# Differential attention: which engine scales which half of the second softmax map, and in what order

## What is computed

```python
sc = einsum('bqhmd,bkhmd->bmhqk', q, k) * scale + bias     # m = 0, 1: two maps
p = softmax(sc, axis=-1)
a = p[:, 0] - lam * p[:, 1]
o = einsum('bhqk,bkhd->bqhd', a, v)
```

## Time and profile before

| | us |
|---|---|
| median of 3 executions | 4073.03 |
| lowest, highest | 4069.45, 4078.59 |
| the profiled execution, whole | 4074.67 |
| its span on the core | 4072.9 |

### The profile page before, as it was taken

One profiled execution on the slowest core, in us unless ns is written; L12 is line 12 of the kernel. 1 busy time (PEld: TensorE's weight loads), 2 busy tenths in 40 slices (PEclk: granted clock), 3 DMA queues, 4 the chain that ended last, 5 costly groups with the idle time before them and its releaser, 6 DMA issues. The chain is left out here.

```text
span 4072.9 us, 51499 instructions
## 1 busy us (share of the span) xinstructions
PE 3784.2 (93%) x19002; PEld 2622.2 (64%) x19002; DVE 2239.3 (55%) x3967; ACT 1658.5 (41%) x2882; POOL 2472.6 (61%) x1385
## 2 busy tenths in 40 slices
PE   8999999999989999789989999999999898997898
PEld 8788774555545665557777897755555465565587
DVE  3012125656569999775530021255555799997754
ACT  3112104333358888661031121033333588886610
POOL 1221326877769999755512213277777699996555
PEclk9999999999999999899989999999999999998999
DMA  5333534243220222335353335323322202224253
GB/s 178 124 134 116 161 122 114 67 101 75 61 56 1 56 57 52 79 89 187 129 181 126 129 120 156 127 59 75 74 65 57 56 3 55 56 52 102 81 179 128
DMA packets 179680, 391.38 MB, mean 96 GB/s; under 512 B 17854, under 2 KB 98984, under 8 KB 167784
## 3 DMA queue, kind: packets, MB, share of 16 engines
q1 hardware_dynamic: 178568, 386.70, 33.7%
q10 hardware_dynamic: 864, 1.41, 0.2%
HBM read 254.88 MB, written 135.67 MB: 96 GB/s over the span
## 5 line engine op out<-in xcount | busy, mean ns | idle before, releaser
L1279 POOL TENSOR_TENSOR mla_sum_pool<-mla_sum_pool,mla_probs 128x1024 f32<-128x1024 f32 (+1 forms) x336 | 777.6, 2314 | 209.5 <-ACT mla_probs L1240 184.7
L1297 DVE TENSOR_REDUCE carry_row_max<-psum 128x1 f32<-128x512 f32 x688 | 474.6, 690 | 415.7 <-PE psum L1112 410.9
L1240 ACT ACTIVATE mla_probs<-psum 128x1024 f32<-128x1024 f32 x384 | 373.3, 1021 | 694.2 <-PE psum L1149 689.5
L1589 ACT ACTIVATE diff_probs<-psum,diff_shift 128x1024 f32<-128x1024 f32 x512 | 566.1, 1111 | 186.3 <-DVE diff_shift L1671 180.3
L1664 DVE TENSOR_REDUCE diff_row_max<-psum 128x1 f32<-128x1024 f32 x512 | 611.9, 1218 | 44.5 <-PE psum L1510 37.2
L1536 PE MATMUL psum<-ident,diff_probs 128*128 128x128 f32 x2048 | 330.1, 285 | 105.8 <-DVE diff_turned L1698 72.0
L624 PE MATMUL psum<-in_x_hi,in_w_hi 128*128 128x512 f32 x1024 | 403.9, 394 | 2.7 <-ACT in_mla_val L733 2.7
L624 PE MATMUL psum<-carry_firsts,in_w_hi 128*128 128x512 f32 x1024 | 404.2, 395 | 0.0
L624 PE MATMUL psum<-in_x_hi,in_w_lo 128*128 128x512 f32 x1024 | 401.4, 392 | 0.0
L1536 PEld LDWEIGHTS psum<-ident,diff_probs 128*128 128x128 f32 x2048 | 217.3, 142 | 282.9 <-issue 185.7
L1162 PE MATMUL psum<-mla_probs,mla_v_op 128*64 128x512 f32 x1536 | 374.9, 610 | 0.0
(11 more groups left out here) (209 smaller groups left out, 7407.4 us busy)
## 6 DMA issues: line engine op xcount, KB each, us to landing
in_w_raw<-in_w_in SPq DMA_DIRECT2D x64, 512.0 KB, 3.9
split_d<-in_out SPq DMA_DIRECT2D x64, 512.0 KB, 2.6
raw_d<-in_out SPq DMA_DIRECT2D x32, 512.0 KB, 2.6
mq_d<-in_out SPq DMA_DIRECT2D x48, 256.0 KB, 3.4
mk_d<-in_out SPq DMA_DIRECT2D x48, 256.0 KB, 3.9
carry_firsts<-split_d SPq DMA_DIRECT2D x48, 256.0 KB, 8.0
carry_weights<-split_d SPq DMA_DIRECT2D x48, 256.0 KB, 7.7
carry_weights<-split_d SPq DMA_DIRECT2D x16, 768.0 KB, 17.2
```

Of the source, the lines that this page charges most:

```text
L1240: nc.scalar.activation(probs[:, s % RING, :].rearrange("p (a n) -> p a n", n=CH), psum[:, S0 + 2 * (s % 2):S0 + 2 * (s % 2) + 2, :], ACT.E ...
L1279: nc.gpsimd.tensor_tensor(acc, start, probs[:, s % RING, mine], ALU.add).then_inc(pool_added, 1)
L1297: nc.vector.tensor_reduce(row_max[:, u % 2, qb, n:n + 1], psum[:, sweep_bank(g), :], AX.X, ALU.max).then_inc(maxed, 1)
L1589: nc.scalar.activation(dst[:, half * HALF:(half + 1) * HALF].rearrange("p (a n) -> p a n", n=CH), banks(n, m, half), ACT.Exp, bias=shift[: ...
```

## The change

A constant `SCALED = HALF` sets how many columns ACT scales: 1024, the whole first half, and not 512. POOL has three instructions a unit and not four: it first scales the second half (which needs only `ratio`), then waits for ACT's scaling and adds the first half, then adds the second half. In the last two units POOL scales nothing and waits for ACT, which scales the 1024 columns alone. DVE's ratio of unit n waits for POOL's one multiply and for ACT's scaling of the unit two before.

```diff
--- before.py
+++ after.py
@@ -1394,6 +1394,7 @@
     DRAIN = 4
     LATE = UNITS - 2
     LOADS = 16 * 14
+    SCALED = HALF
     carry, carry_sems = carry
     vecs, lam_loaded = carry["vecs"], carry_sems["lam_loaded"]
     with ctx:
@@ -1593,7 +1594,7 @@
                 def scale(n):
                     act.wait_ge(ratio_ready, n + 1)
                     at = 0 if n < LATE else HALF
-                    first = probs1[:, n % DEEP1, at:at + CH]
+                    first = probs1[:, n % DEEP1, at:at + SCALED]
                     nc.scalar.activation(first, first, ACT.Copy, scale=ratio[:, n % 2:n % 2 + 1]).then_inc(act_scaled, 1)
 
                 def copy(n, c):
@@ -1635,23 +1636,18 @@
 
 
                     pool.wait_ge(ratio_ready, n + 1)
+                    if n < LATE:
+                        third = probs1[:, n % DEEP1, HALF:SEQ]
+                        nc.gpsimd.tensor_tensor(third, third, ratio[:, n % 2:n % 2 + 1].broadcast_to([P, HALF]), ALU.mult
+                                                ).then_inc(times_ratio, 1)
                     at = 0 if n < LATE else HALF
-                    done = 2 * n if n < LATE else LATE + n
-                    second = probs1[:, n % DEEP1, at + CH:at + HALF]
-                    nc.gpsimd.tensor_tensor(second, second, ratio[:, n % 2:n % 2 + 1].broadcast_to([P, HALF - CH]),
-                                            ALU.mult).then_inc(times_ratio, 1)
                     pool.wait_ge(act_scaled, n + 1)
-                    pool.wait_ge(times_ratio, done + 1)
                     nc.gpsimd.tensor_tensor(probs[:, n % DEEP, at:at + HALF], probs[:, n % DEEP, at:at + HALF],
                                             probs1[:, n % DEEP1, at:at + HALF], ALU.add).then_inc(mixed, 1)
-                    if n >= LATE:
-                        continue
-                    third = probs1[:, n % DEEP1, HALF:SEQ]
-                    nc.gpsimd.tensor_tensor(third, third, ratio[:, n % 2:n % 2 + 1].broadcast_to([P, HALF]), ALU.mult
-                                            ).then_inc(times_ratio, 1)
-                    pool.wait_ge(times_ratio, done + 2)
-                    nc.gpsimd.tensor_tensor(probs[:, n % DEEP, HALF:SEQ], probs[:, n % DEEP, HALF:SEQ], third, ALU.add
-                                            ).then_inc(mixed, 1)
+                    if n < LATE:
+                        pool.wait_ge(times_ratio, n + 1)
+                        nc.gpsimd.tensor_tensor(probs[:, n % DEEP, HALF:SEQ], probs[:, n % DEEP, HALF:SEQ], third, ALU.add
+                                                ).then_inc(mixed, 1)
 
                 pool.wait_ge(o_ready, (H - 1) * (NB // 2))
                 pool.wait_ge(mixed, LATE + UNITS)
@@ -1683,7 +1679,8 @@
                     nc.vector.reciprocal(inv1[:, n % 2:n % 2 + 1], totals[:, 1, qb, h:h + 1]).then_inc(inverted, 1)
                     dve.wait_ge(inverted, n + 1)
                     if n >= 2:
-                        dve.wait_ge(times_ratio, 2 * (n - 1))
+                        dve.wait_ge(times_ratio, n - 1)
+                        dve.wait_ge(act_scaled, n - 1)
                     nc.vector.tensor_scalar(ratio[:, n % 2:n % 2 + 1], inv1[:, n % 2:n % 2 + 1],
                                             totals[:, 0, qb, h:h + 1], dots[:, 0:1], ALU.mult, ALU.mult
                                             ).then_inc(ratio_ready, 1)
```

## The result

The changed kernel takes 4087.23 us (median of 7, 4084.1 to 4089.56), against 4073.03 (median of 7, 4069.45 to 4082.24) before: a ratio of 1.0028, 95% interval 1.0018 to 1.0037. It is slower, by 0.18 to 0.37%. The profiled execution took 4084.1 us, its span is 4082.3 (before: 4072.9). Run once more beside other kernels, it took 4086.8 us against 4078.4 of the kernel before, ratio 1.0023 (1.0014 to 1.0032). The median of the kernel before lay between 4073 and 4078 from one set of runs to the next, so differences are told here as ratios within a set, or from the traces. Within a set the longer executions mostly have the lower mean granted TensorE clock over the whole span (kernel before in the last set: 4067.15 us at 0.980, 4083.66 at 0.975); inside the steady part of the stage it is 1.00 in every trace.

What follows compares the result with a forecast made beforehand. POOL set the stage's long-run mean, with a DVE-PE loop of almost the same length. 24.9 us cost less 10.4 relief gave +14.5 on the profiled 4074.7, so 4089.2, or 4088 as a median; range 4082 to 4098.

Steps and rivals of the forecast that it cites:

- The steady part of the sum: First 28 head-sum distances per layer in the differential-attention stage; the whole forecast change, +14.5 us, was placed there.
- The ends: Last three head-sum distances of each layer, where the stage drains; forecast to change by nothing in sum.
- The scaling: ACT's scaling instruction, 1024 columns instead of 512: forecast to grow by 0.43 us, from 727 ns to 1.16 us.
- The idle time ahead of the head sum: Sign on DVE in each odd iteration: 0.3 to 0.4 us idle before L1716, released by ACT's odd half.
- 24.9 us: Cost of ACT's longer scaling delaying DVE's head sum once per odd iteration: 58 x 0.43 us; bounds 18.6 and 42.
- POOL's relief: Gain from POOL losing its 512-column multiply: 10.4 us, 8.4 in the pairs and about 2 at the layers' starts.
- The steps by which it was split over the pairs: Relief in iteration pairs: 0.5 us for the 15.58 us pair, 0.4 and 0.15 for those of 15.80 and 15.83.
- number 3: Waits and drain: in each layer's last two units ACT's 1.16 us replaces POOL's 1.05, +0.1 us each, nothing in sum.
- PE's wait for POOL: Sign in the changed kernel's profile: PE's waits for POOL, 12.0 us in 460 us before, would be gone.
- Even iterations: ACT's 0.43 us longer scaling fits its 0.51 us idle time before the second map's exponential, so costs nothing there.
- Rival B: POOL held everything; only relief stays, 10 us or more, 4063 or less; full form -86 us, 3987; chance 0.10.

Runs made afterwards that it cites:

- POOL's part alone: Changed kernel with ACT scaling only 512 columns, the other 512 of the first half left unscaled, POOL keeping three instructions: 4070.9 us, ratio 0.9989 to the kernel before.
- ACT's part alone: Kernel before with ACT scaling 1024 columns; POOL keeps four instructions, its 512-column multiply moved to second-half columns: 4088.4 us, ratio 1.0032 to the kernel before.

## Why the prediction was right, and where it was not

- The forecast of 4088 us met 4087.2, but partly by chance: the ratio's interval allows 7 to 15 us more than before, and an error of the sum lies in it. The steady part of the sum, +14.5 us, is +14.4 in the traces. The ends, which the sum had at nothing, gave back 6.8 us in them, so the stage is 7.6 us longer, at the lower side of that interval. By the profiled executions the answer to the sum's 4089.2 is 4084.1; but that was the shortest of the changed kernel's seven, at a mean granted clock of 0.979 (before: 0.977), so it too is partly chance.
- The scaling: forecast 1.16 us from 0.85 ns a column between two other shapes, measured 1.154. The idle time ahead of the head sum: forecast 0.3 to 0.4, measured 0.38 on average. A pair pays 0.36 to 0.43 us, 0.41 on average (15.08 to 15.51 for the shortest, 16.06 to 16.47 for the longest), so 24.9 us was a little high: the changed kernel's steady part is 11.4 and 11.6 us longer than that with POOL's part alone, 23.0 in sum.
- POOL's relief: forecast 8.4 us in the pairs and about 2 at the starts; alone it is 8.5 us in the steady part, the starts included, so the 2 were not there. The steps by which it was split over the pairs (0.5, 0.4, 0.15) measured 0.5, 0.55, 0.16.
- But as two terms the sum was only right in one order. Counted from the kernel before, ACT's part alone costs the whole 14.9 us of the steady part (446.6 - 439.2 and 446.8 - 439.3), since part of the 24.9 is hidden while POOL bounds the loop; POOL's part then adds less than 1. The sum is the same, the blame is not.
- The step that failed is number 3, "+0.1 us each, nothing in sum". It compared the lengths of ACT's and POOL's instructions and did not ask what runs beside POOL's: DVE's mixing, though the trace of before had L1705 at 1276 to 3200 ns for one shape. That is 3.7 of the 6.8 us. Nor did it look at PE's granted clock between the last two mixings, 0.77 and 0.65 before, which came out at 1.00: some 3.1 us, of which the runs show the cost and not the cause.
- PE's wait for POOL was forecast as gone; 2.9 us in 7 places remain. Even iterations paid nothing, as forecast: the cost of eight pairs is that of eight longer scalings, not sixteen.
- Rival B, with POOL as the bound, was told apart best by POOL's part alone: 1 to 8 us less than before, where the full form of that rival has 86.

## What to carry to other kernels

An edge between two engines that is met just in time leaves no idle time in the trace: compare the end of each operand with the start of its user, not only the listed waits. Before work is moved from a full engine to one with slack, look at where in its program order it lands, and who waits for what stands behind it; here the kernel gains 0.2% once the head sum stands one copy later and the split is 768 to 256, and 0.4% with the last units' handling, a part of it by a clock that did not fall. Two costs in loops that bound each other do not add, so measure each part both alone and on top of the other. Where a stage ends and PE begins to stand idle, read the granted clock before an end is put down to the work.

## What the runs showed of the hardware

DVE's mixing of two SBUF inputs takes 1.28 us alone, and POOL's sum 2.37. Together, over 12 traces, the one that starts first keeps its length: with the mixing ahead by 0.06 to 0.22 us it takes 1.28 us and the sum 3.26 to 3.42; with the sum ahead by 0.09 to 0.24 us it takes 2.34 or 2.35 us and the mixing 3.18 to 3.33. Beside POOL's multiply, recorded 0.04 or 0.05 us behind it, the mixing takes 2.16 or 2.17 us (512 columns) or 1.74 (256), and the multiply keeps its 1.04 or 0.61. In the loop itself, where DVE reads PSUM, POOL's sums stay at 2.37 us.

TensorE's granted clock fell in 16 of 24 ends of the stage: after 2.27 us of idle time in both layers the same eight products took 1.98 us in one layer and 1.08 in the other, in one execution of one kernel. At its full level that stretch takes 5.9 us, with a granted clock of 0.77 it takes 7.4 to 7.5.
